# Row sums of the full softmax tiles: VectorE additions in place of four 32-column matmuls

## The reference

```python
def _fox_prompt(q, k, v, logf):              # 12 heads of 128, S = 2048, blocks of queries
    cum = jnp.transpose(jnp.cumsum(logf, axis=1), (0, 2, 1))
    ...
    s = jnp.einsum('bqhd,bkhd->bhqk', qi, k).astype(jnp.float32) * scale
    s = s + ci[..., :, None] - cum[:, :, None, :]
    s = jnp.where(k_pos[None, :] <= pi[:, None], s, NEG_INF)
    p = jax.nn.softmax(s, axis=-1).astype(v.dtype)
    return jnp.einsum('bhqk,bkhd->bqhd', p, v)
```

## Time and profile before

| | |
|---|---|
| median of three runs | 3167.25 us |
| the profiled execution: its own time | 3169.76 us |
| its span (slowest core, core 4) | 3168.2 us |
| spans of the cores | 3132.6 to 3168.2 us |
| busy over the span: PE, DVE, ACT, POOL | 98%, 56%, 31%, 20% |
| attention, 1709.7 to 2349.4 us: PE, DVE, ACT, POOL busy | 621.4, 382.3, 471.0, 331.5 of 639.7 us |
| merge products alone, 2349.4 to 2463.3 us: PE, DVE busy | 113.9, 0.7 of 113.9 us |

### The profile page before, as it was taken

How to read it: one execution, slowest core, us unless ns; L and a number is a source line. 1 busy time by engine, 2 the same in 40 slices (tenths; PEclk the granted TensorE clock), 3 DMA queues, 4 the chain that set the end, 5 groups by cost and what they waited for, 6 DMA issues and landing times.

```text
span 3168.2 us, 57364 instructions; the slowest of 8 cores (3132.6 to 3168.2 us)
## 1 busy us (share of the span) xinstructions
PE 3100.9 (98%) x20146; PEld 1933.3 (61%) x20245; DVE 1764.9 (56%) x2677; ACT 990.2 (31%) x1652; POOL 631.0 (20%) x804
## 2 busy tenths in 40 slices
PE   6999999999999999999998999999999999999997
PEld 4566666666666666666665555555556666666443
DVE  5634444455567787777554565665530344444665
ACT  1222222222221111111324777777751211111111
POOL 2000000000011212111002455555431010000233
PEclk9889999999999999999999999999999999999999
DMA  9457777653445555432549987878755986667753
GB/s 164 97 102 177 185 182 187 150 137 86 113 94 80 88 82 88 72 55 52 128 132 183 209 175 203 188 203 178 176 166 150 288 219 164 172 157 233 259 188 114
DMA packets 245697, 481.44 MB, mean 152 GB/s; under 512 B 75900, under 2 KB 138636, under 8 KB 238616
## 3 DMA queue, kind: packets, MB, share of 16 engines
q0 software_dynamic: 50736, 174.53, 32.4%
q1 hardware_dynamic: 189624, 274.12, 28.5%
q10 hardware_dynamic: 5056, 29.10, 2.6%
HBM read 441.82 MB, written 180.58 MB: 196 GB/s over the span
## 4 chain that ended last, share of the span: by engine, by line
PE 94%; DMA 3%; issue 1%; DVE 1%; ACT 0%; POOL 0%; SPq 0%; another core or an unknown queue 0%; DVEq 0%; ACTq 0%; POOLq 0%
PE bank L148 93%; DMA g_scr<-o4c 1%; PE bank L1560 1%; DMA xT<-xT 1%; DMA mq<-mq_scr 1%; DMA wo<-wf_scr 1%; DMA a_scr<-ao 0%; DMA cqb<-cum_scr 0%; SPq L157 0%; DVE x L183 0%; ACT o4c L165 0%; DVE st L183 0%; ACT pt L165 0%; SPq L848 0%; DVE acc L175 0%
## 5 line engine op out<-in xcount | busy, mean ns | idle before, releaser
L148 PE MATMUL bank<-xT,ring 128*128 128x352 bf16 x6144 | 1035.8, 314 | 9.4 <-ACT pt L165 3.9
L148 PEld LDWEIGHTS bank<-xT,ring 128*128 128x128 bf16 x6144 | 597.0, 98 | 350.2 <-issue 16.3
L148 PE MATMUL bank<-xT,ws 128*128 128x352 bf16 x3072 | 498.7, 316 | 23.7 <-DMA xT<-xT 23.7
L148 PE MATMUL bank<-xs,ring 128*128 128x352 bf16 x3072 | 497.9, 316 | 0.1
L175 DVE TENSOR_TENSOR s<-bank,t 128x704 f32<-128x704 f32 x192 | 171.0, 890 | 521.4 <-PE bank L148 383.3
L148 PE MATMUL bank<-a,wo 128*128 128x352 bf16 x3072 | 458.7, 313 | 1.0 <-DMA wo<-wf_scr 0.5
L148 PEld LDWEIGHTS bank<-xT,ws 128*128 128x128 bf16 x3072 | 302.8, 99 | 186.5 <-issue 25.6
L148 PEld LDWEIGHTS bank<-xs,ring 128*128 128x128 bf16 x3072 | 302.9, 99 | 163.5 <-issue 1.5
L170 ACT ACTIVATE t<-bank 128x704 f32<-128x704 f32 x192 | 144.8, 754 | 820.9 <-PE bank L148 820.9
L148 PEld LDWEIGHTS bank<-a,wo 128*128 128x128 bf16 x3072 | 300.4, 98 | 159.1 <-issue 1.6
L175 DVE TENSOR_TENSOR tr<-bank,g 128x704 f32<-128x704 f32 x144 | 128.4, 892 | 339.8 <-PE bank L148 338.4
(11 more groups left out here) (163 smaller groups left out, 2901.2 us busy)
## 6 DMA issues: line engine op xcount, KB each, us to landing
ring<-w_in POOLq DMA_DIRECT2D x112, 512.0 KB, 8.9
g<-g_scr SPq DMA_DIRECT2D x144, 352.0 KB, 4.8
g_scr<-gst POOLq DMA_DIRECT2D x96, 352.0 KB, 6.2
ring<-w_merge POOLq DMA_DIRECT2D x48, 512.0 KB, 8.5
x<-xp SPq DMA_DIRECT2D x16, 1024.0 KB, 5.9
y_p<-x SPq DMA_DIRECT2D x14, 1024.0 KB, 4.1
xT<-xT POOLq DMA_DIRECT2D x36, 352.0 KB, 22.9
a<-a_scr ACTq DMA_DIRECT2D x6, 2112.0 KB, 10.9
```

The lines of the kernel that those rows point to most:

```text
L148: return lambda e: e.matmul(out, lhsT=lhsT, rhs=rhs, start=start, stop=stop)
```

## The change

The full tiles are no longer summed on TensorE. For each block VectorE adds the first two `pt` tiles into `acc`, then every further one to `acc` (f32 plus bf16), and multiplies `acc` by `fq` in SBUF. In a head that is 3, 7 and 11 additions for blocks 1, 2 and 3, so 21, and 252 in 12 heads; the 288 matmuls in 72 groups of four go, with the constant `ones32`. The bank of `PJ_p` that held the sums is not taken.

```diff
-    ones32 = C0.tile("ones32", [128, 32], BF16, [r_const])
...
         if offs:
-            for t in offs[0:4]:
+            held = None
+            for t in offs:
                 yield wait(t.exp)
-            bk, rb = yield get(PJ_p)
-            for g in range(0, len(offs), 4):
-                for t in offs[g:g + 4]:
-                    yield wait(t.exp)
-                yield op(PE, 1, t_pe(512) + 0.05, [
-                    (lambda e, o_=bk[32 * k:32 * k + 32, :], p=t.p[0], g=g, k=k: e.matmul(
-                        o_, lhsT=ones32[:, :], rhs=p[:, :], start=g == 0, stop=g == len(offs) - 4, tile_position=(0, 32 * k)),
-                     [r_const, t.p[1]], [rb]) for k, t in enumerate(offs[g:g + 4])])
-                for t in offs[g:g + 4]:
-                    t.ref.drop()
+                if t.kc == 0:
+                    held = t
+                    continue
+                src, rsrc = (held.p if held is not None else b.acc)
+                yield op(DVE, 2, t_dvs(512), [(TT(ac[:, :], src[:, :], t.p[0][:, :], ALU.add), [rsrc, t.p[1]], [rac])], 0.3)
+                if held is not None:
+                    held.ref.drop()
+                    held = None
+                t.ref.drop()
             yield wait(b.fqe)
             fq, rfq = b.fq
-            yield op(DVE, 1, t_dve(512), [(TT(ac[:, :], bk[:, :], fq[:, :], ALU.mult), [rb, rfq], [rac])], 0.3)
-            L.put(PJ_p, (bk, rb))
+            yield op(DVE, 2, t_dvs(512), [(TT(ac[:, :], ac[:, :], fq[:, :], ALU.mult), [rac, rfq], [rac])], 0.3)
             b.fqref.drop()
```

More of the change, by code:

```diff
@@ L549, in build @@
     S.add(DVE, lambda e: e.memset(ones1[:], 1.0), writes=[r_const])
-    S.add(DVE, lambda e: e.memset(ones32[:], 1.0 / 32), writes=[r_const])
     S.add(DVE, lambda e: e.memset(epsb[:], LN_EPS), writes=[r_const])
```

## The result

The kernel after the change takes 3143.17 us (median of 4; 3138.38 to 3148.52) against 3168.51 us of the kernel before in the same comparison: ratio 0.9922, 95% interval 0.9901 to 0.9943, which is 25 us less. Two more comparisons of the same two kernels gave 0.9912 (0.9893 to 0.9931) and 0.9932 (0.9908 to 0.9955). I had forecast 12 us more. The time lies in my range and on the side to which I gave 0.29. (The ratios compare undisturbed executions on one chip; medians of single runs in later comparisons contain disturbed ones and are not used.)

The account below looks back on a forecast made before the run. TensorE, busy 98%, bounds the kernel; afterwards VectorE paces the attention at 734 us, +94.3, less 82.5 of merge products no longer behind it: +12 on 3167.25, 3179 us (chance 0.42). Range for 8 in 10: 3138 to 3210.

Parts of the forecast that it names:

- the side to which I gave 0.29: Whole kernel: chance that the change makes it faster by more than the 6.3 us a measurement can tell.
- What goes from TensorE: Row-sum matmuls in the attention: 72 groups of four at 0.42 us each leave TensorE, 30.2 us.
- What moves on TensorE: 552 merge products, 82.5 us, move into the attention; TensorE's work there becomes 673.7 us, the stretch 692.0 with 18.3 idle.
- What VectorE gets: Attention: 252 additions at 898 ns (226.3 us), 3.9 for SBUF products, 11.4 for the chain; VectorE's work 623.9 us.
- What of it lies beside other work: VectorE's waits in the attention: 96.4 us and 14 us of small gaps stay, so its 734 us set the attention's length.
- Behind the attention: Remaining 216 merge products (32 us) and output stage start: nothing counted, bounds -0.46 and 5.6 us.
- TensorE stays the bound: Rival: additions fill VectorE's 62.7 us wait for `rl` in the attention, 30.2 us saved, 3137 us; chance 0.30.
- They cancel: Rival: additions fill 12 of the 62.7 us, TensorE idles the 30 us it was relieved of, 3167 us; chance 0.13.
- GpSimd and VectorE block each other: Rival: SBUF additions in the attention wait longer meeting GpSimd's instructions; half of 54 us added, 3206 us; chance 0.15.
- What would show it: Signs in the attention: TensorE some 60 us idle, stretch about 734; idle staying near 18 us would prove the prediction wrong.

Follow-up runs that it names:

- e2: Kernel after, same list order, without the third and later additions of a block (216 of 252); ratio to the kernel before 0.9902, 6 us below the kernel after.
- e6: Kernel after, same list order, plus an unrelated 128-column maximum of constants on VectorE behind each of 252 additions; ratio to the kernel before 0.9998.
- e9: Kernel after plus the unrelated 128-column maximum on VectorE behind only 144 of 252 additions; ratio to the kernel before 0.9963.
- e10: Kernel after without the low part of the split of acc (60 GpSimd subtractions and 60 onesb matmuls left out); ratio to the kernel before 0.9894.
- e3: Kernel after, same list order, plus a 128-column maximum of acc with itself behind each of block 2's 84 additions; ratio to the kernel before 0.9968.
- e4: Kernel after, same list order, plus a 128-column maximum of acc with itself behind all 252 additions; ratio to the kernel before 1.0171.
- e5: Load of e4 on the kernel after, with the scheduler told 0.45 us more per addition, so another list; ratio to the kernel before 1.0241.
- e1: Kernel before with each group of four row-sum matmuls issued twice, same list order; ratio to the kernel before 1.0041, 13 us more.

## Why the prediction was wrong

**What goes from TensorE: right.** 72 groups of 0.42 us, 30.2 us; e2 measures 31, and the stage itself is some 34 us shorter there.

**What moves on TensorE: right, in part by luck.** 676.6 us of work in the attention against 673.7, and 32.7 us of merge products behind it against 32. But both the work (621.4) and the idle time (18.3) that I began with came from a record that lacks 77 matmuls in the attention. From core 1 the work would have been 626.2 - 30.2 + 82.5 = 678.5 us, and the idle time 12.2; the two errors nearly cancel.

**What VectorE gets: the price of an addition was right, the sum 33 us too high.** 891 ns against 898. But VectorE's busy time rose by 590.9 - 382.3 = 208.6 us, not 241.6. Three things make the difference. The 11.4 us for the chain are waiting and no work in the trace, and there are fewer of them: `acc` behind `acc` is 6.4 us in 37 waits, where it was 3.6 in 21. The recorded times of all VectorE groups together rose by 225 us, where I had 230. And recorded times overlap, by some 16 us more than before: an instruction starts some 0.08 us before the record of the one before it ends, as the earlier trace rows showed (0.60 from start to start at 0.68 recorded). I had used that as the lower end of the range and not in the sum. Busy time counts such laps once, so what is added to it must be a distance between starts.

**What of it lies beside other work: wrong, and this is the step that failed.** I let 96.4 us of VectorE's waits and 14 us of small gaps stand, added them to its work as if they were work, and let the 734 us so made pace the attention. VectorE does not pace it: without 174 us of its work (e2) the kernel is only 6 us faster. The largest of the waits, 62.7 us for the reciprocal, was 2.6 us afterwards; e2 shows that the additions fill this time, since without them `on` waits 66.7 us again. And under load (e6) 52.5 us of idle time remain, not 110. 591 us of work with that idle time would be 643 us, less than the 690 that the attention takes with TensorE. That sum is no bound either: e9 has 630.8 + 52.5 = 683 us by it, below 690 too, and costs 10 to 13 us. My row for this was a sum of waits of an engine that was not the bottleneck, and most of it did not have to stand.

The 99 us that VectorE still idles in the kernel after look much like the 110 that I let stand; e6 shows that about half of them can be filled. So a better number would have proved nothing here: with VectorE's measured busy time, 590.9 + 110.4 = 701 us, the same wrong step gives 21 us less, near the measured 25, by luck.

**Behind the attention: right in size.** I counted nothing, between -0.46 and 5.6; it is 2 to 3 us, and the one wait shown, 2.26 us, is for VectorE's `tr` and not for a load.

**The rivals.** "TensorE stays the bound" (0.30, 3137 us) is what happened, by its own condition: the additions fill the wait for `rl`. The measured 25 us are 5 short of its 30.2: e2 puts about 6 us on the additions and 2 to 3 lie behind the attention, while the groups were worth a little more. "They cancel" had the same condition to a fifth and is out. "GpSimd and VectorE block each other" is out in the form in which I priced it: the additions wait no longer than before. The blocking is there, but it went to the other side. GpSimd's groups of two forms in the attention, first before the change, then after it:

```profile
L175 POOL TENSOR_TENSOR hl<-acc,hl 128x512 bf16<-128x512 f32 x47 | 54.1, 1159 | 2.5 <-PE bank L148 0.4 <-POOL hl L171 0.4 <-PE bank L1560 0.2
L171 POOL CAST hl<-acc 128x512 bf16<-128x512 f32 x47 | 28.3, 614 | 46.7 <-DVE acc L175 43.9 <-PE bank L148 2.8
```

```profile
L175 POOL TENSOR_TENSOR hl<-acc,hl 128x512 bf16<-128x512 f32 x47 | 59.1, 1259 | 3.1 <-POOL hl L171 0.6
L171 POOL CAST hl<-acc 128x512 bf16<-128x512 f32 x47 | 34.5, 735 | 64.2 <-DVE acc L175 44.1 <-PE bank L148 19.7 <-DVE st L183 0.3
```

The subtraction takes 1259 ns on average and not 1159, the cast 735 and not 614; in e2, with most additions out, they are at 1186 and 655. What this alone costs no run shows; as far as the additions cause it, it lies within the 6 us of e2. The Trainium skill (SBUF — State Buffer, section "Who interferes with whom") says that a VectorE instruction with two SBUF inputs contends with a GpSimd instruction that reads SBUF, and that the port pair which they share is an exclusive lock. That GpSimd's instructions become longer with the additions agrees with it, and e10 shows the other half: fewer GpSimd instructions, shorter additions.

**What would show it.** I had written that TensorE's idle time staying near 18 us would mean that the 30.2 us are simply saved. It is 13.8, and on whole records it rose only from 7.0 to 11.5 on average.

## What to carry to other kernels

Here one engine was saturated, a list scheduler laid the work, and moving 72 groups from it to an engine with 40% idle time paid nearly their whole price. The present waits of the second engine, added up, did not tell what it could take: most of them were where it had nothing else to do. Measure what it can take by loading it in an unchanged order (e3, e4, e6, e9), and take work away from it (e2) to see whether it paces. Expect a price that grows, not a threshold, and a higher one where the work hangs in the chain. And keep some filler work behind the stage: the list that spent it too early cost 22 us on top of the load's 79 (e5).

Before two profiles are compared, compare the counts: a record that lacks matmuls shows idle time that is not there.

## What the runs showed of the hardware

Four 128x32 matmuls of 512 columns, each in its own columns, take 0.22 us together right behind another such group, as long as one full matmul of 512 columns (e1); a group that stands alone among full matmuls costs 0.42. GpSimd's instructions are longer where VectorE adds more in SBUF, and the additions shorter where GpSimd does less: GpSimd's cast of 512 columns takes 614 ns before, 735 after and 655 in e2; the addition 891 ns after and 811 in e10, whose list is another one. In the 100 us in which e5's TensorE was 73% busy its granted clock was 0.80 on average, and a matmul of 512 columns is recorded with 0.59 us at 2400.92 and with 0.38 at 2405.53, so the window holds both levels (1.2 and 2.4 GHz); in the same kernel the clock was 1.00 in 100 us at 97%.
